# A decoder block's kernel: the order of VectorE's work at the last expert, and of ScalarE's in one attention step

## The chip, the cores and the metric

The kernel runs on one core of a Trainium2 chip. The core has five engines that run programs of their own and meet at semaphores: TensorE (matrix products and transposes), VectorE, ScalarE, GpSimd, and SyncE, which here only issues DMAs. The metric is the time of one execution on the device in microseconds; of several executions the median counts.

## The reference

One layer of a decoder on 512 tokens of width 1024 in float32, then a final normalisation:

```python
h = rms_norm(x, norm_mix) * (1 + sc1) + sh1
x = x + g1 * hybrid_mixer(h, ...)      # four head groups, then @ w_out
h = rms_norm(x, norm_ffn) * (1 + sc2) + sh2
x = x + g2 * hier_moe(h, ...)          # 16 experts, two for each token
out = rms_norm(x, final_norm)
```

The mixer's groups are sliding-window attention (`swa`), causal pooling, an attention with compressed, selected (`sel`) and windowed (`win`) branches, and a gated delta rule. Each expert computes `silu(t @ w_gate) * (t @ w_up)`, times the routing weight, `@ w_down`, with 1024 x 512 weights; a token's two experts are chosen by top-k and the two results are added to the token's row.

## The kernel before, in words

P is 128, ST is 4 (the 512 tokens are four tiles of 128 rows). Each engine's program is written out by hand, in order. An engine waits at `wait_ge` and holds all that stands behind it in its program. `Link` adds a semaphore to an instruction and makes the same engine wait for it.

**The attention** runs in steps s = 0 to 27. A step is one pair of heads and one tile of queries: eight `swa` steps, then sixteen `sel` and `win` steps. At step s TensorE makes the scores of pair s (`pe_attention_step`, L670 and the masks L677), transposes the probabilities of pair s - 2 (L692) and multiplies those of pair s - 3 with the values (L713). VectorE takes the maxima of pair s (L744) and scales the probabilities of pair s - 1 (L769, L772). ScalarE, in `act_attention_step`, makes the exponentials of pair s (L796, L797) and then copies the transposed probabilities of pair s - 2 from PSUM into `pTr` (L809), signalling `pT_out`.

Between steps 9 and 10 (`CMP_TRANSPOSES = 10`) TensorE transposes the probabilities of the compressed branch, `cn` (`pe_cmp_transposes`, L636). They go into the bank that the transposes of the eight `swa` pairs used, so TensorE waits for `pT_out` of all of them, of which the last is copied in ScalarE's step 9. It also waits for `cn`, which VectorE makes (L627). ScalarE copies the result out as `pTc` ahead of its step 10 (`act_cmp_evict`, L641), and TensorE's transposes of the first `sel` pair wait for that. `pe_cmp_values` (L651) uses it at step 11.

**The experts** follow the output projection (L1207) and the routing. Experts are in an order `ORDER`, with n = 0 to 15; they get 128, 64 or 32 rows each, the last three 32. For each n TensorE makes gate and up products (`pe_gate_up`: L1050 for 128 rows, L1044 for fewer), ScalarE applies silu (`act_silu`, L1123, into `sg`), VectorE multiplies with the up half (`dve_product`, L1156 or L1158, into `hidm`), TensorE transposes it (L1060), ScalarE copies it (`act_hidden`, L1128, into `hidT`), and TensorE makes the down products (`pe_down`, L1083 or L1078) with the weights `dn`. Weights come by DMAs that SyncE issues in `sync_moe` (gate and up L913 or L981, down L916) as the three buffers come free. The down weights of the last expert are issued when the down products of the thirteenth (n = 12) are done.

The outputs of experts 0 to 12 are scaled on VectorE and stored to `expert_rows` in HBM. GpSimd gathers them back by token: `y1`, four DMAs that signal `y1_in` together, and `y2`, four DMAs with a signal each (L1701). VectorE adds them, each row times its routing weight, onto `x2` (`rows_added`, L1625, one 128 x 1024 instruction a tile). The outputs of the last three experts stay on the chip: `dve_output` writes them into `yc` (L1172, four pieces), and TensorE's `pe_back` (L1102) multiplies `yc` with a matrix `back` that sends rows to tokens, two halves of 512 columns for each tile. VectorE adds these onto `x2` (L1646), ScalarE squares and sums the tile (L1412) and takes the root (L1414), VectorE scales it (L1676, L1677), and SyncE stores it (L1005), waiting for the stores at the end.

In the loop over experts before the change, VectorE did this for the last one (n = 15): `dve_output` of n = 14, `rows_added` of all four tiles of `y1` and of two of `y2`, `dve_product` of n = 15, the other two tiles of `y2`, and then `dve_output` of n = 15.

Of the kernel before, what the change touches and what calls it, by code (L numbers as in the profile page):

```python
# [45 lines left out]
E = G * EG  # L46
# [215 lines left out]
def build(nc, A, out):  # L262
# [63 lines left out]
    def sem(name):  # L326

        if name not in sems:
            sems[name] = ctx.enter_context(nc.semaphore(name))
        return sems[name]  # L330
# [177 lines left out]
    def pair_heads(kind, pr):  # L508
        return (pr, pr + 2) if kind == "swa" else (2 * pr, 2 * pr + 1)

    def pair_keys(kind, i):

        j0 = max(i - 1, 0) if kind == "swa" else 0
        return j0, (i + 1 - j0) * P
# [260 lines left out]
    Y_DONE = {ST - 1: (0, YBANKS[0]), 2 * ST - 1: (1, YBANKS[1]), 2 * ST + 7: (4, YBANKS[0]), 2 * ST + 15: (5, YBANKS[1])}  # L775
    NUN = 2 * NPS

    def act_attention_step(act, s):
        a = nc.scalar
        if s < NPS:  # L780
            kind, pr, i = pairs[s]
            nk = pair_keys(kind, i)[1]
            for b, n in enumerate(SCORES[s]):
                u = 2 * s + b
                act.wait_ge(sem("max"), u + 1)
                if s >= 2 and b == 0:

                    act.wait_ge(sem("prob"), 2 * (s - 2) + 2)
                if u >= PRS:

                    act.wait_ge(sem("prob_tr"), u - PRS + 1)
                c = 2 * (s % 2) + b
                m = nm[:, c:c + 1]
                if kind == "swa":
                    h = pair_heads(kind, pr)[b]
                    a.activation(esk[:, c:c + 1], sinkb[:, h:h + 1], ACT.Exp, bias=m)  # L796
                a.activation(T["pr"][:, u % PRS, 0:nk], PS[n][:, 0:nk], ACT.Exp, bias=m,  # L797
                             accum_out=den[:, c:c + 1]).then_inc(sem("exp"), 1)
        if TR_LAG <= s < NPS + TR_LAG:
            w = s - TR_LAG  # L800
            kind, pr, i = pairs[w]
            nk = pair_keys(kind, i)[1]
            if w >= 2:

                act.wait_ge(sem("pv_mm"), w - 1)
            for b in range(2):
                act.wait_ge(sem("prob_tr"), 2 * w + b + 1)
                nb = nk // P
                a.activation(T["pTr"][:, w % 2, b, 0:nb, :].rearrange("p j c -> p (j c)"), PROBS[b][:, 0:nk],  # L809
                             ACT.Copy).then_inc(sem("pT_out"), 1)  # L810

    def pe_pool_products(pe, c):

        t = nc.tensor
        pe.wait_ge(sem("wr_in"), 96)
        pe.wait_ge(sem("pool_d"), 2 * c + 2)
        for b in range(2):
            pb = slice(HD * b, HD * b + HD)
            ins = t.matmul(YBANKS[c][pb, :], T["wpool"][pb, c, :], T["pd"][pb, c, :], start=True, stop=True)
        ins.then_inc(sem("pool_mm"), 1)  # L820
# [22 lines left out]
    CMP_SCORES, CMP_IN, CMP_OUT, CMP_TRANSPOSES, CMP_VALUES = 7, 7, 8, 10, 11  # L843
# [49 lines left out]
    def rows_of(n):  # L893
        return SIZES[ORDER[n]] if n < E else P

    def small(n):
        return rows_of(n) < P

    def on_chip(n):
        return E - CHIP <= n < E  # L900

    def down_bank(n):
        return 5 if n == E - 2 else 4
# [237 lines left out]
    def dve_rows(dve, n):  # L1141
        if n:
            dve.wait_ge(sem("mod_moved"), 48)
        scale, shift = (rA, rshift) if n else (A2, mod[:, 24:32])
        dve.wait_ge(sem("xg_tr"), n + 1)
        m = rows_of(n)
        for k in range(4, KT):
            ins = nc.vector.tensor_scalar(T["xgT"][:, k, 0:m], PS[7][:, (k - 4) * m:(k - 3) * m], scale[:, k:k + 1],  # L1148
                                          shift[:, k:k + 1], ALU.mult, ALU.add)
        ins.then_inc(sem("xgT_d"), 1)  # L1150

    def dve_product(dve, n, b):
        dve.wait_ge(sem("sg"), n + 1)
        if small(n):
            f = F * rows_of(n) // P
            ins = nc.vector.tensor_tensor(T["hidm"][:, 0:f], T["sg"][:, 0:f], PS[2 * b][:, f:2 * f], ALU.mult)  # L1156
        else:
            ins = nc.vector.tensor_tensor(T["hidm"][:], T["sg"][:], PS[2 * b + 1][:, :], ALU.mult)  # L1158
        ins.then_inc(sem("hidm"), 1)

    def dve_output(dve, n):

        dve.wait_ge(sem("g2_moved"), 1)
        dve.wait_ge(sem("dn_mm"), n + 1)
        if on_chip(n):

            dve.wait_ge(sem("yo_d"), E - CHIP + 1)
            dve.wait_ge(sem("xg_tr"), E)
            to = slice(32 * (n - E + CHIP + 1), 32 * (n - E + CHIP + 2))
            for w in range(4):  # L1170
                rows, c = slice(32 * w, 32 * w + 32), slice(256 * w, 256 * w + 256)
                ins = nc.vector.tensor_tensor(T["yc"][to, c], PS[down_bank(n)][rows, 0:256], T["g2q"][rows, :],  # L1172
                                              ALU.mult)
            ins.then_inc(sem("yo_d"), 1)
            return
        dve.wait_ge(sem("yo_st"), 16 * STORED[n])
        if small(n):
            d = D * rows_of(n) // P
            g = {512: T["g2s"], 256: T["g2q"]}[d]
            ins = nc.vector.tensor_tensor(T["yo"][:, 0:d], PS[4][:, 0:d], g[:], ALU.mult)  # L1180
        else:
            for w in range(2):
                c = slice(w * 512, (w + 1) * 512)
                ins = nc.vector.tensor_tensor(T["yo"][:, c], PS[4 + w][:, :], T["g2m"][:, c], ALU.mult)  # L1184
        ins.then_inc(sem("yo_d"), 1)
# [230 lines left out]
    def dve_moe(dve):  # L1416
# [200 lines left out]
        def rows_added(n, tiles=range(ST)):  # L1617

            if n == 0:
                dve.wait_ge(sem("y1_in"), 16 * ST)  # L1620
            for i in tiles:
                x = T["x2"][:, i, :]
                if n:
                    dve.wait_ge(sem(f"y_in{i}"), 16)
                ins = v.scalar_tensor_tensor(x, T[f"y{n + 1}"][:, i, :], (w1, w2)[n][:, i:i + 1], x, ALU.mult, ALU.add)  # L1625
            link(ins)

        for n in range(1, E):
            if n == E - 1:
                dve_output(dve, n - 1)  # L1630
                rows_added(0)
                rows_added(1, (0, 1))
            dve_product(dve, n, n % 2)
            if n == E - 1:
                rows_added(1, (2, 3))
            if n + 1 < E:
                dve_rows(dve, n + 1)
                dve_output(dve, n - 1)
            if n == E - 2:
                v.memset(T["yc"][0:32, :], 0.0)  # L1640
        dve_output(dve, E - 1)
        for i in range(ST):
            dve.wait_ge(sem("oproj_mm"), ST + 1 + i + 1)
            for w in range(2):
                x = T["x2"][:, i, w * 512:(w + 1) * 512]
                ins = v.tensor_tensor(x, PS[2 * i + w][:, :], x, ALU.add)  # L1646
            ins.then_inc(sem("x3"), 1)
# [279 lines left out]
    def _(act):  # L1927
# [97 lines left out]
        for s in range(STEPS):  # L2025
            if s == CMP_TRANSPOSES:
                act_cmp_evict(act)
            act_attention_step(act, s)
            if s == HIDDEN_EXP:
                act.wait_ge(sem("gate_in"), 1)  # L2030
                a.activation(gate, gate, ACT.Exp, scale=-1.0).then_inc(sem("scalars"), 1)
                act_compress(act)
            if s == CMP_IN:
                act_cmp_exp(act)
# [5 lines left out]
    def _(dve):  # L2040
# [265 lines left out]
        for s in range(STEPS):  # L2306
# [24 lines left out]
            if s == CMP_OUT:  # L2331
                dve_cmp_softmax_out(dve)
        dve_moe(dve)

    @block.tensor
# [302 lines left out]
```

## Time and profile before

| | us |
|---|---|
| median of 3 runs | 772.02 |
| lowest and highest | 770.45, 775.83 |
| the profiled execution | 771.39 |
| its span, first to last instruction | 769.6 |
| busy in the span: TensorE, VectorE, ScalarE, GpSimd | 682.3, 328.8, 180.2, 116.6 |
| mean granted TensorE clock | 0.957 |

Times in the rows are microseconds from the start of the span. In a row of the chain or of the timeline the first number is the start, the second the length; "x4" counts instructions. A float32 product shows as two or more instructions. "Granted clock" is TensorE's clock as a share of 2.4 GHz; 0.50 is the lower of its two levels, 1.2 GHz.

### The profile page before, as it was taken

To read this page: it belongs to the slowest core of one execution; us is meant where nothing else is said; L and a number is where in the kernel's file an instruction comes from. 1 tells how busy PE (TensorE), PEld (TensorE's weight loads), DVE (VectorE), ACT (ScalarE), POOL (GpSimd) and SP (SyncE) were. 2 spreads that over 40 slices of the span, in tenths; PEclk is the share of its full clock that TensorE was granted. 3 is DMA by queue.
4 is the path that set the end of the run, shared out by engine and by line. 5 is a ranking of instruction groups with operands and counts; after the bars stand their busy time and mean duration, and the time that the engine had idled before them with its cause. 6 is when DMAs were issued, how large, how long until landed. Compare 5 with 4: busy or idle time off the path is not lost.

```text
span 769.6 us, 9939 instructions
## 1 busy us (share of the span) xinstructions
PE 682.3 (89%) x3865; PEld 397.2 (52%) x3869; DVE 328.8 (43%) x782; ACT 180.2 (23%) x435; POOL 116.6 (15%) x164
## 2 busy tenths in 40 slices
PE   1699899999999999887999994899999999999544
PEld 1574346667666598555554554445443444444211
DVE  2203757856467433585723228562111121212355
ACT  3204315122121121455721113111111121111113
POOL 8700122314032057000000000000000000000300
PEclk9999999999999899898999996999999999999977
DMA  9999103793330120850062117998999999999962
GB/s 330 374 258 377 16 1 110 245 311 114 110 110 1 22 35 2 273 187 34 1 219 55 55 37 261 410 327 287 392 403 395 422 397 418 387 413 403 421 261 111
DMA packets 76239, 172.90 MB, mean 225 GB/s; under 512 B 21890, under 2 KB 39004, under 8 KB 72860
## 3 DMA queue, kind: packets, MB, share of 16 engines
q1 hardware_dynamic: 70912, 157.85, 56.6%
q0 software_dynamic: 2608, 9.18, 3.2%
q10 hardware_dynamic: 2668, 5.18, 1.8%
q8 instruction: 33, 0.54, 0.3%
q14 instruction: 18, 0.15, 0.1%
HBM read 156.33 MB, written 15.87 MB: 224 GB/s over the span
## 4 chain that ended last, share of the span: by engine, by line
PE 75%; DVE 11%; POOL 4%; DMA 3%; issue 3%; ACT 3%; POOLq 0%; DVEq 0%; ACTq 0%
PE ps L1050 13%; PE ps L1207 7%; PE ps L2463 7%; PE ps L1083 6%; PE ps L2430 5%; PE ps L1044 5%; PE ps L2541 2%; DMA y<-expert_rows,slot 2%; PE ps L1078 2%; PE ps L2547 2%; PE ps L2427 2%; PE ps L2454 2%; POOL lev L1805 2%; PE ps L2551 2%; PE ps L670 2%
## 5 line engine op out<-in xcount | busy, mean ns | idle before, releaser
L1050 PE MATMUL ps<-gu,xgT 128*128 128x512 f32 x224 | 97.4, 593 | 3.4 <-DVE xgT L1148 2.3
L2463 PE MATMUL ps<-hT,winr 128*128 128x512 f32 x144 | 73.2, 617 | 0.2
L1689 POOL DMA_INDIRECT xg<-xn_rows,list x15 | 13.9, 927 | 381.5 <-PE ps L1019 183.6
L1050 PEld LDWEIGHTS ps<-gu,xgT 128*128 128x128 f32 x224 | 42.0, 190 | 54.1 <-issue 54.1
L1044 PE MATMUL ps<-gu,xgT 128*32 128x256 f32 (+1 forms) x416 | 52.1, 487 | 8.0 <-DMA gu<-in_w_up 8.0
L1207 PE MATMUL ps<-wout,yT 128*128 128x512 f32 x128 | 56.3, 595 | 0.0
L1916 POOL TENSOR_TENSOR cc<-low,lev 128x512 f32<-128x512 f32 x20 | 30.2, 1518 | 131.1 <-DVE low L2250 105.6
L1083 PE MATMUL ps<-dn,hidT 128*128 128x512 f32 x112 | 49.4, 594 | 0.0
L2054 DVE SCALAR_TENSOR_TENSOR acc<-ada,st,acc 128x512 f32<-128x512 f32 x56 | 48.5, 866 | 1.3
L2430 PE MATMUL ps<-hT,wind 128*128 128x512 f32 x96 | 42.3, 594 | 0.0
L1123 ACT ACTIVATE sg<-ps 128x512 f32<-128x512 f32 (+2 forms) x16 | 7.2, 450 | 134.8 <-PE ps L1050 90.5
L1207 PEld LDWEIGHTS ps<-wout,yT 128*128 128x128 f32 x128 | 23.9, 190 | 27.9 <-issue 27.9
L1044 PEld LDWEIGHTS ps<-gu,xgT 128*32 128x32 f32 (+1 forms) x416 | 19.5, 127 | 36.1 <-issue 23.5
L1158 DVE TENSOR_TENSOR hidm<-sg,ps 128x512 f32<-128x512 f32 x7 | 4.8, 686 | 68.6 <-ACT sg L1123 68.6
L1083 PEld LDWEIGHTS ps<-dn,hidT 128*128 128x128 f32 x112 | 20.7, 190 | 23.5 <-issue 23.4
L2463 PEld LDWEIGHTS ps<-hT,winr 128*128 128x128 f32 x144 | 24.4, 195 | 14.7 <-issue 12.7
L744 DVE TENSOR_REDUCE st<-ps 128x1 f32<-128x256 f32 (+3 forms) x48 | 20.4, 452 | 19.0 <-PE ps L677 19.0
L2430 PEld LDWEIGHTS ps<-hT,wind 128*128 128x128 f32 x96 | 17.9, 190 | 20.2 <-issue 20.1
L1078 PE MATMUL ps<-dn,hidT 128*32 128x256 f32 (+1 forms) x208 | 27.4, 498 | 0.7 <-ACT hidT L1128 0.7
L2349 PE MATMUL ps<-ada,st 128*32 128x128 f32 x256 | 11.2, 341 | 18.6 <-DMA ada<-in_w_ada 17.5
L2264 DVE TENSOR_TENSOR uu<-uu,ps 128x512 f32<-128x512 f32 x20 | 13.7, 687 | 32.8 <-PE ps L2547 32.8
L1128 ACT ACTIVATE hidT<-ps 128x512 f32<-128x512 f32 (+2 forms) x16 | 7.2, 451 | 85.4 <-DVE yo L1184 50.5
(451 smaller groups left out, 1083.9 us busy)
## 6 DMA issues: line engine op xcount, KB each, us to landing
dn<-in_w_down SPq DMA_DIRECT2D x16, 2048.0 KB, 20.6
gu<-in_w_gate SPq DMA_DIRECT2D x14, 2048.0 KB, 13.9
gu<-in_w_up SPq DMA_DIRECT2D x14, 2048.0 KB, 19.2
ada<-in_w_ada SPq DMA_DIRECT2D x12, 2048.0 KB, 12.0
expert_rows<-zero SPq DMA_DIRECT2D x12, 512.0 KB, 6.6
gu<-in_w_gate SPq DMA_DIRECT2D x8, 512.0 KB, 5.0
gu<-in_w_up SPq DMA_DIRECT2D x8, 512.0 KB, 6.5
expert_rows<-yo ACTq DMA_DIRECT2D x7, 512.0 KB, 10.5
```

Source lines behind the costliest of these rows:

```text
L670: t.matmul(PS[n][:, 0:nk], q[pb, pr, i * P:(i + 1) * P], keys[pb, 0, j0 * P:j0 * P + nk], start=True, stop=False)
L744: ins = v.tensor_reduce(m, PS[n][:, 0:nk], AX.X, ALU.max, negate=True)
L1044: ins = nc.tensor.matmul(PS[2 * b][m * s:m * s + m, 0:2 * f].rearrange("p (w f) -> p w f", w=2), T["xgT"][:, k, 0:m], w_in[:, :, k, s * f: ...
L1050: ins = nc.tensor.matmul(PS[2 * b + w][:, :], T["xgT"][:, k, :], w_in[:, w, k, :], start=(k == 0), stop=(k == KT - 1))
L1078: ins = nc.tensor.matmul(PS[down_bank(n)][m * w:m * w + m, 0:d], T["hidT"][:, c, m * s:m * s + m], w_in[:, f, w * d:(w + 1) * d], start=(f ...
L1083: ins = nc.tensor.matmul(PS[4 + w][:, :], T["hidT"][:, f, :], w_in[:, f, w * 512:(w + 1) * 512], start=(f == 0), stop=(f == FT - 1))
L1207: ins = nc.tensor.matmul(PS[2 * (i % 2) + n][:, :], T["yT"][:, k, i * P:(i + 1) * P], T["wout"][:, k, n * 512:(n + 1) * 512], start=(k == ...
L1805: link(g.affine_select(out=t, in_=t, pattern=pattern, compare_op=op, fill=fill, base=base, channel_multiplier=cm))
L1916: g.tensor_tensor(CC[lv % 2][:], T["low"][:], T["lev"][:, lv].unsqueeze(1).broadcast_to([P, H, P]), ALU.mult).then_inc(sem("cc"), 1)
L2054: ins = v.scalar_tensor_tensor(o, piece[:, k, :], csil[:, k:k + 1], o, ALU.mult, ALU.add)
L2430: ins = t.matmul(bank[:, :], w(k), T["hT"][:, k, :], start=(k == 0), stop=(k == KT - 1))
L2463: ins = t.matmul(bank[:, :], w(k), T["hT"][:, k, :], start=(k == 0), stop=(k == KT - 1))
```

## The change

ScalarE's attention step is split in two functions, exponentials and copies. Their order is as before in all steps but step 9 (`CMP_TRANSPOSES - 1`), where the copies come first.

On VectorE the last expert's product comes right after the output of expert 14. Tiles 0 and 1 of `y1` are added after it, before the last expert's output; tiles 2 and 3 of `y1` after that output; and each tile of `y2` just ahead of that tile's products from `pe_back`.

```diff
-    def act_attention_step(act, s):
+    def act_exps(act, s):
         a = nc.scalar
         if s < NPS:
...
                 a.activation(T["pr"][:, u % PRS, 0:nk], PS[n][:, 0:nk], ACT.Exp, bias=m,
                              accum_out=den[:, c:c + 1]).then_inc(sem("exp"), 1)
+    def act_prob_copies(act, s):
+        a = nc.scalar
         if TR_LAG <= s < NPS + TR_LAG:
             w = s - TR_LAG
             kind, pr, i = pairs[w]
...
+
+    def act_attention_step(act, s):
+
+        if s == CMP_TRANSPOSES - 1:
+            act_prob_copies(act, s)
+            act_exps(act, s)
+        else:
+            act_exps(act, s)
+            act_prob_copies(act, s)
...
         for n in range(1, E):
             if n == E - 1:
                 dve_output(dve, n - 1)
-                rows_added(0)
-                rows_added(1, (0, 1))
             dve_product(dve, n, n % 2)
-            if n == E - 1:
-                rows_added(1, (2, 3))
             if n + 1 < E:
                 dve_rows(dve, n + 1)
                 dve_output(dve, n - 1)
             if n == E - 2:
                 v.memset(T["yc"][0:32, :], 0.0)
+        rows_added(0, (0, 1))
         dve_output(dve, E - 1)
+        rows_added(0, (2, 3))
         for i in range(ST):
+            rows_added(1, (i,))
             dve.wait_ge(sem("oproj_mm"), ST + 1 + i + 1)
             for w in range(2):
                 x = T["x2"][:, i, w * 512:(w + 1) * 512]
```

## Rows read from the trace of the kernel before

**Rows 1.** The page: DMA share in 40 slices of the span, the chain by engine.

```profile
DMA  9999103793330120850062117998999999999962
...
PE 75%; DVE 11%; POOL 4%; DMA 3%; issue 3%; ACT 3%; POOLq 0%; DVEq 0%; ACTq 0%
```

**Rows 2.** The chain of waits, attention, steps 8 to 12: start, length, what.

```profile
346.41 0.76 DVE cn L627 x2
...
349.26 0.56 ACT pTr L809 x2
...
349.95 1.09 PE ps L636 x4
...
352.09 1.71 PE ps L692 x8
...
356.81 1.24 PE ps L651 x8
...
360.14 0.23 PE ps L692 x2
```

**Rows 3.** The timeline of the same stretch: start, length, what, idle before it and its releaser.

```profile
345.32 0.68 PE L692 MATMUL ps<-idf,pr 128*128 128x128 f32 x4 [0.83 <-ACT pTr L809]
345.94 0.66 PE L713 MATMUL ps<-pTr,va 128*64 128x128 f32 x8
...
348.48 1.00 DVE L772 TENSOR_SCALAR pr<-pr,st 128x512 f32<-128x512 f32 x2
...
351.07 0.60 ACT L641 ACTIVATE pTc<-ps 128x512 f32<-128x512 f32 x1 [1.27 <-PE ps L636]
```

**Rows 4.** Stretches of the attention: busy PE, PEld, DVE, ACT, POOL; granted clock, DMA share, GB/s.

```profile
349.00:350.00 1.00, 0.05 (x1) 0.08 (x2) 0.48 (x2) 0.80 (x4) 0.00 (x0) 0.51 0.00 0
350.00:355.00 5.00, 5.00 (x28) 3.79 (x30) 1.56 (x5) 2.49 (x7) 0.00 (x0) 0.50 0.01 2
```

**Rows 5.** The chain of waits at the end.

```profile
744.24 0.30 DVE hidm L1156
```

**Rows 6.** Timelines of the end, by engine, columns as in rows 3.

```profile
720.55 1.93 PE L1078 MATMUL ps<-dn,hidT 128*32 128x256 f32 x32 [0.36 <-ACT hidT L1128]
...
736.30 0.28 ACT L1123 ACTIVATE sg<-ps 128x128 f32<-128x128 f32 x1 [15.81 <-PE ps L1044]
736.82 4.87 DVE L1625 SCALAR_TENSOR_TENSOR x<-y,w1t,x 128x1024 f32<-128x1024 f32 x4 [12.14 <-DMA y<-expert_rows,slot]
...
745.42 3.37 PE L1078 MATMUL ps<-dn,hidT 128*32 128x256 f32 x32 [0.37 <-ACT hidT L1128]
...
749.02 1.73 DVE L1172 TENSOR_TENSOR yc<-ps,g2q 32x256 f32<-32x256 f32 x4 [2.10 <-issue]
...
759.73 1.29 DVE L1646 TENSOR_TENSOR x<-ps,x 128x512 f32<-128x512 f32 x2 [0.43 <-PE ps L1102]
```

**Rows 7.** The chain of waits later in the attention, at a granted clock of 1.00.

```profile
375.54 0.59 PE ps L713 x8
376.13 0.42 PE ps L670 x4
376.55 0.22 PE ps L677 x2
376.77 0.88 PE ps L692 x8
377.65 1.02 PE ps L713 x16
378.67 0.85 PE ps L670 x4
```

**Rows 8.** The timeline of SyncE: the issue of the last down weights.

```profile
713.64 0.38 SPq L916 DMA_DIRECT2D dn<-in_w_down  x1
```

**Rows 9.** DMA issues between 713.5 and 714.0: KB, us from issue to landing.

```profile
dn<-in_w_down SPq DMA_DIRECT2D x1, 2048.0 KB, 26.6
```

**Rows 10.** A stretch of the end, columns as in rows 4.

```profile
741.00:742.00 1.00, 0.00 (x0) 0.00 (x0) 0.96 (x2) 0.00 (x0) 0.00 (x0) 0.78 1.03 410
```

## The prediction

> **What bounds the kernel now.** I read the chain of waits first. TensorE has three quarters of it and VectorE a tenth [rows 1]; so an edit on VectorE or ScalarE pays only where TensorE stands waiting for that engine. The change touches two such places, far apart, and the reader should look at each on its own.
>
> The first is the step of the attention before TensorE's transposes of the compressed probabilities. In the chain [rows 2] TensorE's four transposes (L636) start at 349.95, released by ScalarE's two copies (L809), which ended at 349.82. Their other input, `cn`, was finished by VectorE at 346.41 + 0.76 = 347.17. The probabilities that the copies move had been transposed by 345.32 + 0.68 = 346.00 [rows 3]. ScalarE held the copies back because its program has the exponentials of that step ahead of them, and these waited for maxima. TensorE's pause made its clock fall: granted 0.51 in the microsecond from 349, and 0.50 from 350 to 355 [rows 4], the lower of its two levels (1.2 against 2.4 GHz).
>
> The second is the end. The chain [rows 5] has the product `hidm` of the last expert at 744.24, though its input `sg` was ready at 736.30 + 0.28 = 736.58 [rows 6]. Between them VectorE added gathered rows `y`, from 736.82, when the first of them had landed. Then come TensorE's down products at 745.42, `yc` on VectorE until 749.02 + 1.73 = 750.75, the products that send rows back to their tokens, the last addition until 759.73 + 1.29 = 761.02, the final scalings and the stores. From 761.02 to the end of the span (769.6) are 8.58 us, which the change leaves alone.
>
> **Part one: copies before exponentials in one step.** Nothing is added or removed; ScalarE exchanges two exponentials and two copies at step 9. The copies need the transposes that ended at 346.00. Moved up they run while ScalarE waits for maxima, and by their own 0.65 us or so are over near 346.7, a microsecond before the exponentials can begin. So the exponentials keep their time, and no queue of DMAs is passed.
> TensorE's L636 can then start at about 347.2, when `cn` is there: 2.7 us earlier. What is late next? The transposes of the selected probabilities (L692, behind L636 and two score products) wait for ScalarE's copy `pTc`. That copy stands in ScalarE's queue behind step 9's exponentials, which end where the copies began, at 349.26 [rows 2]. It takes 0.60 us [rows 3], so L692 starts at about 350.0. VectorE's probabilities for it are done by 348.48 + 1.00 = 349.5 [rows 3]. Before, L692 followed its predecessors in TensorE's queue at 352.09 by the chain, or 351.9 with the overlap of single records. That is 1.9 us, and it is carried on, since TensorE works without a gap from there to 360.14.
> There is more if the clock stays up. The work from L692 to the row at 360.14 is, by the same shapes at the full clock [rows 7] : transposes 0.88, values 0.59, scores 0.42 + 0.22, transposes 0.88, the compressed values 1.24 (the row at 356.81 in [rows 2], run mostly after the clock had risen), values 1.02, scores 0.85 + 0.22: together 6.3 us, so 356.3 instead of 360.14, a gain of 3.8 us. The other engines follow: ScalarE's exponentials of step 10 and its copies, and VectorE's maxima and scalings, each come out ready before TensorE asks. Does it stay up? TensorE stopped at 345.94 + 0.66 = 346.6 [rows 3], and a granted 0.51 from 349 to 350 means that the clock fell at about 349.0, after 2.4 us of standing still. With the change the pauses are 0.6 us (346.6 to 347.2) and 1.5 us (about 348.5 to 350.0). I take the full clock, 3.8 us, and keep 1.9 as the bound. The lowest bound is 0, if the 1.9 us were lost to a wait that I do not see; a loss has no row, since ScalarE idles where the copies go. After this place all waits are between engines that move together: the output products, the routing, and the loads of expert weights, which SyncE issues on signals of TensorE and VectorE. So the gain arrives at the end whole.
>
> **Part two: the product first.** VectorE does the same 8 additions of gathered rows, one product, four pieces of `yc`, and 8 half additions. Only their order changes.
> Removed from the path: the additions between 736.82 and 744.24. The product could start at 736.6. From product to down products were 745.42 - 744.24 = 1.18 us, so TensorE could begin them at 737.8.
> A new wait takes the place: the down weights of the last expert. Their DMA was issued at 713.64 [rows 8] and landed 26.6 us later [rows 9], at 740.24. Before, that was hidden. Now the down products start at about 740.3, 5.1 us earlier than before and not 7.6.
> Their length depends on the clock. The same 32 products took 1.93 us at 720.55 and 3.37 us at 745.42 [rows 6], the latter at the lower level: in the trace the clock fell to it between 741 and 742 [rows 10], some 5.3 us after the last gate and up product, which ended as `sg` began. In the new order one transpose (0.3 to 0.5 us) comes at about 737.0 and then 2.8 us without work, close to the 2.4 us after which the clock fell in the attention and well under the 5.3 us here. Rows leave this open, so I take the middle of the two.
> From the end of the down products to the end of `yc` were 750.75 - 748.79 = 1.96 us. So `yc` is ready at 740.3 + 1.93 + 1.96 = 744.2, or at 740.3 + 3.37 + 1.96 = 745.6; before 750.75.
> Now the additions that used to lie ahead stand behind: two of the first rows (1.22 us each, 4.87 for four in [rows 6]), then for each of four tiles one of the second rows (1.22 too, and some 0.06 for the waits around a single one) and two halves (1.29). 2 x 1.22 + 4 x (1.22 + 0.06 + 1.29) = 12.7 us, all on VectorE, one after another. TensorE's back products all fell in the 10.3 us from `yc` to the last addition, so VectorE becomes the bound of the tail. Two additions of first rows are hidden in the wait for the weights. Before, `yc` to the last addition took 761.02 - 750.75 = 10.3 us; it will take 2.4 us more, because six additions of rows are behind it.
> End of the span for this part alone: 744.2 + 12.7 + 8.6 = 765.5 or 745.6 + 12.7 + 8.6 = 766.9, against 769.6: a gain of 4.1 or 2.7, middle 3.4. ScalarE's squares (about 1.1 us a tile) keep up with 2.6 us a tile. Its table load at 745.6 moves forward with `hidT` and is off the path.
>
> By the Trainium skill (TensorE: Matmul & The Clock Gate, Part 1) the gate judges TensorE's activity on a schedule that runs on its own and does not begin with the kernel, so the place of a fall differs between executions. The two falls here (2.4 and 5.3 us after the last work) agree with that. If so, the tail's clock is a draw in each execution rather than one value. Its two outcomes are those priced above, 765.5 and 766.9.
>
> **Sum.** 3.8 + 3.4 = 7.2 us. The profiled execution took 771.39 us for its span of 769.6; it should become 762.4 in the span and 764.2 in all. The median of the runs shown, 772.02, is 0.6 above it, so I forecast 764.8.
>
> **Rivals.**
> (A) As above, 763.4 to 765.9 with the clock and small hops. Chance 0.58.
> (B) The clock falls in the attention all the same, so that part brings 1.9: 766.7. For it: TensorE still works only about half of the time between 344.4 and 350. Against it: no single pause is as long as that of before. 0.17.
> (C) The edit in the attention does not do what it says, because L636 or L692 is held by something that the copies hid: 0 + 3.4, 768.6. For it: only a last releaser is shown. Against it: `cn` was there at 347.17. 0.12.
> (D) DMA is the pace of the expert stage and not TensorE. The DMA engines are at nine tenths and more from routing on [rows 1], and nothing of what they move gets less. The attention's gain is then used up in waits for weights, and the last down weights may come when the old down products began, 745.4, or later. Then `yc` is done at 750.75 as before, with 12.7 us behind it where 10.3 were: 772.02 + 2.4 = 774.4, slower. The tail turns into a loss once the down products start after 769.6 - 8.6 - 12.7 - 1.96 - 3.37 = 743.0. Against it: SyncE issues each load on a release, which comes earlier with the rest; the landing would have to slip by 2.7 us. 0.05.
> (E) In most executions the last down weights land before 737.8, so nothing holds them: 2.4 us more, 762.4. For it: I have one execution. 0.08.
>
> **How the numbers follow.** A measurement of this kernel can tell about 1% (7.7 us) from no change, so the forecast lies almost on that line, 764.3. A has about two fifths of its chance under it, E all of its own, B a little through the scatter of runs (770.45 to 775.83): faster 0.36. Slower by over 1% needs D and more: 0.04. The rest, 0.60, is within 1%. The range: 761.8 (E, with some scatter) to 768.9 (C), which leaves out D, the far side of E and part of C.
>
> **What would show it.** In the profile after: ScalarE's copies of step 9 at about 346 and L636 at about 347.2; L692 at about 350; granted clock 1.00 through 350 to 355 (B: 0.50); everything from L1207 on 3.8 us earlier. At the end, in distances: the product within 0.1 us of `sg`; TensorE's down products 3 to 4 us after the end of the last gate and up products, released by the DMA of `dn`; the half additions one after another on VectorE with no idle time, about 2.6 us a tile, while TensorE is done before. If the down products start 1.2 us after `sg`, E holds. If L1207 starts at 391.6 as before, C does. The prediction goes wrong above all if the landing of the last down weights moves against TensorE's work, for each microsecond there is one of the result.

## The result, and the profile after

Over 20 executions of each the changed kernel took 768.12 us (median; 762.40 to 772.09), the kernel before 773.49 (766.13 to 777.91). The ratio is 0.9945, with a 95% interval of 0.9927 to 0.9964: 4.2 us less, between 2.8 and 5.6. The forecast was 7.2 less. The profiled execution of the changed kernel took 767.23 us, span 765.4, against 771.39 and 769.6. Lines of the changed kernel from L797 on have other numbers (L809 is now L811, L1207 is L1218, L1078 is L1089).

The attention first: the chain of waits of the changed kernel (start, length, what), against [rows 2].

```profile
343.52 0.76 DVE cn L627 x2
...
346.37 0.50 ACT pTc L641
...
347.00 1.06 PE ps L692 x8
...
353.57 0.23 PE ps L692 x2
```

And its timeline, with the moved copies (343.22) and TensorE's transposes of `cn`:

```profile
343.22 0.66 ACT L811 ACTIVATE pTr<-ps 128x256 f32<-128x256 f32 x2 [0.65 <-PE ps L692]
...
344.34 0.65 PE L636 MATMUL ps<-idf,cn 128*128 128x128 f32 x4 [0.41 <-DVE cn L627]
```

The copies are over before VectorE has finished `cn`, L636 starts 0.06 us after it (before: 2.78 us after), and L692 waits for `pTc`, as worked out. From the end of `cn` to the row that was at 360.14 were 12.97 us, and now are 9.29: 3.68 less. The clock stayed up; busy PE, PEld, DVE, ACT, POOL, then the granted clock, in the stretch where [rows 4] has 0.50:

```profile
350.00:355.00 5.00, 5.00 (x52) 2.92 (x52) 2.44 (x9) 2.23 (x8) 0.00 (x0) 1.00 0.01 3
```

Now the end, in the timelines of VectorE and TensorE of the changed kernel, against [rows 6]:

```profile
735.23 0.29 DVE L1167 TENSOR_TENSOR hidm<-sg,ps 128x128 f32<-128x128 f32 x1 [9.72 <-ACT sg L1134]
735.44 2.48 DVE L1636 SCALAR_TENSOR_TENSOR x<-y,w1t,x 128x1024 f32<-128x1024 f32 x2
742.34 1.73 DVE L1183 TENSOR_TENSOR yc<-ps,g2q 32x256 f32<-32x256 f32 x4 [4.42 <-issue]
...
755.49 1.29 DVE L1656 TENSOR_TENSOR x<-ps,x 128x512 f32<-128x512 f32 x2
...
728.67 6.17 PE L1055 MATMUL ps<-gu,xgT 128*32 128x256 f32 x64 [5.33 <-DMA gu<-in_w_up]
735.58 0.33 PE L1071 MATMUL ps<-idf,hidm 128*128 128x128 f32 x1 [0.73 <-DVE hidm L1167]
738.49 3.64 PE L1089 MATMUL ps<-dn,hidT 128*32 128x256 f32 x32 [2.58 <-issue]
744.21 8.72 PE L1113 MATMUL ps<-yc,back 128*128 128x512 f32 x16 [2.09 <-DVE yc L1183]
```

The row to look at is the one at 738.49. The product follows `sg` at once, but TensorE stands idle for 2.58 us between its transpose of `hidm` and the down products. "Issue" names no one: the profile sees no engine that released them. Their weights had been issued at 711.79, and the view of DMA issues gives 26.6 us to landing, 738.4. `yc` is done at 744.07, and then VectorE works without a pause to 755.49 + 1.29 = 756.78.

Both local forecasts hold in what happens, and nearly in size, and yet the sum does not. The ledger of the two profiles, in us, from the starts and ends of the same instructions:

| distance | before | after | less |
|---|---|---|---|
| start of the span to the end of `cn` | 347.17 | 344.28 | 2.89 |
| `cn` to the first product of the output projection | 44.41 | 40.74 | 3.67 |
| from there to the issue of the first down weights | 68.28 | 69.98 | -1.70 |
| to the first expert's gate and up products | 26.98 | 26.97 | 0.01 |
| to the last expert's gate and up products | 243.68 | 246.70 | -3.02 |
| to VectorE's last addition | 30.50 | 28.11 | 2.39 |
| to the end of the span | 8.58 | 8.62 | -0.04 |
| sum | 769.6 | 765.4 | 4.20 |

The -0.04 in the last row is rounding: the spans are given to a tenth. The first row has identical code in both kernels and cannot be the change's. The clock's falls lie elsewhere in the two executions: granted 0.54 from 260 to 264 us before and 1.00 after, 0.52 and 0.83 from 315 to 322. The third and fifth are losses in places that the edit does not touch, and they need an explanation. In the timeline of the changed kernel the first expert's products take 16.99 us, where the kernel before has 13.97:

```profile
481.97 16.99 PE L1061 MATMUL ps<-gu,xgT 128*128 128x512 f32 x32 [2.06 <-DVE xgT L1159]
```

```profile
486.84 13.97 PE L1050 MATMUL ps<-gu,xgT 128*128 128x512 f32 x32 [2.32 <-DVE xgT L1148]
```

The windows of the changed kernel show the granted clock (third number from the end) in the output projection and in these products:

```profile
436.00:437.00 1.00, 1.00 (x6) 0.74 (x6) 0.26 (x2) 0.64 (x3) 0.00 (x0) 0.93 0.00 0
437.00:440.00 3.00, 3.00 (x4) 1.01 (x3) 1.05 (x1) 0.00 (x0) 0.00 (x0) 0.50 0.37 147
440.00:441.00 1.00, 1.00 (x3) 0.49 (x2) 0.00 (x0) 0.00 (x0) 0.00 (x0) 0.87 0.25 98
...
481.00:487.00 6.00, 5.03 (x6) 2.18 (x7) 5.59 (x27) 0.00 (x0) 1.19 (x1) 0.52 0.97 410
```

TensorE's products run on in both, at half its clock: 3.4 us at the lower level in the projection cost 1.7, some 6 us in the expert's products cost 3.0. In the profile of the kernel before the clock is 1.00 in both places.

### The profile page after: what moved, and what is told of

Read it like the earlier page. It is cut to its first block, busy times and chain, and to the rows that moved or that the text cites. A ratio compares the mean times of both kernels' runs of the same rounds, so it can differ in the third digit from the quotient of the medians.

```text
span 765.4 us, 9942 instructions
## 1 busy us (share of the span) xinstructions
PE 686.4 (90%) x3865; PEld 397.8 (52%) x3869; DVE 330.2 (43%) x782; ACT 180.7 (24%) x435; POOL 116.8 (15%) x164
## 4 chain that ended last, share of the span: by engine, by line
PE 75%; DVE 11%; POOL 4%; issue 3%; DMA 3%; ACT 3%; SPq 0%; POOLq 0%; DVEq 0%; ACTq 0%
PE ps L1061 13%; PE ps L1218 7%; PE ps L2473 7%; PE ps L1094 6%; PE ps L1055 6%; PE ps L2440 5%; DMA gu<-in_w_up 3%; PE ps L2551 2%; PE ps L2557 2%; PE ps L1089 2%; PE ps L2437 2%; PE ps L2464 2%; POOL lev L1815 2%; PE ps L670 2%; PE ps L2561 2%
## 5 line engine op out<-in xcount | busy, mean ns | idle before, releaser
L1061 PE MATMUL ps<-gu,xgT 128*128 128x512 f32 x224 | 100.5, 608 | 3.1 <-DVE xgT L1159 2.1
L1218 PE MATMUL ps<-wout,yT 128*128 128x512 f32 x128 | 58.0, 610 | 0.0
L1218 PEld LDWEIGHTS ps<-wout,yT 128*128 128x128 f32 x128 | 24.4, 195 | 29.0 <-issue 29.0
L1089 PE MATMUL ps<-dn,hidT 128*32 128x256 f32 (+1 forms) x208 | 29.3, 504 | 3.8 <-issue 3.2
L1167 DVE TENSOR_TENSOR hidm<-sg,ps 128x256 f32<-128x256 f32 (+1 forms) x9 | 3.3, 362 | 58.5 <-ACT sg L1134 58.5
L1441 DVE TENSOR_TENSOR x<-ps,g1b 128x512 f32<-128x512 f32 x8 | 5.5, 689 | 49.3 <-PE ps L1218 49.3
## 6 DMA issues: line engine op xcount, KB each, us to landing
gu<-in_w_gate SPq DMA_DIRECT2D x14, 2048.0 KB, 13.2
```

Of the source, the lines that this page charges most:

```text
L1061: ins = nc.tensor.matmul(PS[2 * b + w][:, :], T["xgT"][:, k, :], w_in[:, w, k, :], start=(k == 0), stop=(k == KT - 1))
L1089: ins = nc.tensor.matmul(PS[down_bank(n)][m * w:m * w + m, 0:d], T["hidT"][:, c, m * s:m * s + m], w_in[:, f, w * d:(w + 1) * d], start=(f ...
L1218: ins = nc.tensor.matmul(PS[2 * (i % 2) + n][:, :], T["yT"][:, k, i * P:(i + 1) * P], T["wout"][:, k, n * 512:(n + 1) * 512], start=(k == ...
```

## The experiments

"Faster" and "less" are against executions of the kernel before that were taken beside those of the run, unless said. One microsecond is 0.0013 of the ratio.

**The two edits apart** (`e1_copies_only`, `e2_product_only`): each takes one hunk of the diff alone.

> The attention's edit alone (copies ahead of exponentials in step 9, VectorE's order as before). Theory T1, terms as predicted: 3.8 us less than before, ratio about 0.995. Theory T2, clock draws: the 1.9 us from waits are there in every execution, but the further 1.9 us need that the kernel before has its fall of the clock in that pause; over many executions that holds in part, and the time is 2 to 3 us less, ratio 0.996 to 0.9975. Rival T3, the expert stage eats it: 0 to 1 us. In the profile under T1 and T2: TensorE's transposes of cn start when cn is done, and the span between cn and the output projection is shorter by 3.5 us than in the profile of before, at a full clock.

Measured: 768.18 against 771.16; ratio 0.9955 (0.9930 to 0.9980), 3.5 us less. The distance from `cn` to the projection is 40.75 in its profile. The expectation's T1 fits the median; the interval holds T2 as well, and shuts T3 out.

> VectorE's edit alone (product of the last expert first, step 9 of ScalarE as before). Theory: down products start when the last down weights land, VectorE then has 12.7 us from yc to the last addition: 2.4 to 2.7 us less than before with the low clock in the down products, 4.1 with the full clock; ratio 0.9945 to 0.997. Rival: the serial additions cost all that the earlier product brings, 0 us. If the two edits add, the ratio of this run and that of the other edit give together 0.9945, the ratio of the whole change.

Measured: 769.65; 0.9974 (0.9947 to 1.0001), 2.0 us less, not clear of zero by itself. The two together would be 0.9929, the whole change 0.9945 (0.9927 to 0.9964): they add, within what can be told. The new tail is not all VectorE's either: with the back products at the low clock from start to end (10.09 us) TensorE held up two of the half additions, and from `yc` to the last addition it took 13.2 us and not 12.7. The old tail is itself not one number. In the first run, with VectorE's old order, the gate and up products to the last addition took 28.88 us and not 30.50, because TensorE's back products ran at the full clock from the start:

```profile
749.23 7.10 PE L1113 MATMUL ps<-yc,back 128*128 128x512 f32 x16 [2.10 <-DVE yc L1183]
```

**More additions ahead** (`e3_five_ahead`), to see whether VectorE is the bound of the tail:

```diff
-        rows_added(0, (0, 1))
+        rows_added(0)
+        rows_added(1, (0,))
         dve_output(dve, E - 1)
-        rows_added(0, (2, 3))
         for i in range(ST):
-            rows_added(1, (i,))
+            if i:
+                rows_added(1, (i,))
```

> The changed kernel, but all four tiles of y1 and the first of y2 are added in the wait for the last down weights, so three additions (3.7 us) leave the stretch behind yc. Theory (VectorE bounds the tail): 2 to 3 us less than the changed kernel, because TensorE's back products then become the bound at about 10.3 us from yc to the last addition, as before the change; against before 6 to 7 us less, ratio 0.991 to 0.992. Rival (the tail is bound by something else, or yc is delayed by the additions ahead): no gain over the changed kernel, ratio 0.9945, or a loss of 1 us.

Measured: 767.12; 0.9942 (0.9918 to 0.9966). No gain over the changed kernel; the expectation was wrong. The timeline of VectorE shows why:

```profile
742.11 1.73 DVE L1183 TENSOR_TENSOR yc<-ps,g2q 32x256 f32<-32x256 f32 x4 [0.63 <-PE ps L1089]
747.67 1.29 DVE L1657 TENSOR_TENSOR x<-ps,x 128x512 f32<-128x512 f32 x2 [3.83 <-PE ps L1113]
748.88 1.28 DVE L1636 SCALAR_TENSOR_TENSOR x<-y,w2t,x 128x1024 f32<-128x1024 f32 x1
```

The time saved behind `yc` became a wait of 3.83 us for TensorE's first back products, and three additions of `y2` still stood between the half additions after it. From the start of the back products to the last addition it took 12.52 us, and 12.57 in the changed kernel. VectorE and TensorE each bound pieces of this tail.

**A lighter load of the last down weights** (`e4_light_down`):

```diff
-                load_down(sp, expert[n - 1], (n - 1) % NBUF)
+                if n == E:
+                    sp.dma_start(dn[..][:, 0:1], wd_v[expert[n - 1]][:, 0:1]).then_inc(..)
+                else:
+                    load_down(sp, expert[n - 1], (n - 1) % NBUF)
```

> The changed kernel with only the first quarter of the last expert's down weights loaded (the other three quarters are left out, so the last expert computes with old weights there). Theory (the landing of these weights starts the down products): they start 1.2 us after sg instead of 3.5 us, and the time is 2.2 to 2.5 us less than that of the changed kernel, ratio to before about 0.9915. Rival (down products wait for something else on ScalarE or VectorE): they start as late as in the changed kernel, and the ratio stays at 0.9945.

Measured: 763.82; 0.9917 (0.9883 to 0.9950). In its profile the down products are released by ScalarE's `hidT`, with no other wait, 1.44 us after the gate and up products and not 3.65:

```profile
737.02 1.93 PE L1093 MATMUL ps<-dn,hidT 128*32 128x256 f32 x32 [0.37 <-ACT hidT L1143]
```

The last gate and up products to the last addition took 23.99 us instead of 28.11. Of these 4.1 us 2.2 are the wait, and 1.7 the down products, which ran at the full clock. Over executions it is 2.1 us less than the changed kernel, by the ratios. The landing was the wait.

**TensorE kept at work in the tail** (`e5_busy_tail`): `pe_busy(n)` issues n spare transposes of 128x128 into a bank that nobody reads.

```diff
         pe_hidden(pe, E - 1, 1)
+        pe_busy(20)
         pe_down(pe, E - 1)
+        pe_busy(15)
```

> The changed kernel with 20 spare transposes on TensorE between the last expert's hidden transposes and its down products, and 15 between down products and back products, into a bank that nobody reads. Theory (the clock falls in these pauses and nothing else in the tail is sensitive to it): the down products take 1.9 us instead of 3.6, so yc and the end come 1.7 us sooner than in the changed kernel; the back products get shorter too (8.8 to 7 us), which brings nothing, as VectorE's additions are the bound. Ratio to before about 0.9925. Rival (the fall has another reason, or the spare work delays the down products): ratio 0.9945 or more.

Measured: 764.19 against 770.68; 0.9920 (0.9894 to 0.9945). Down products 1.93 us, back products 7.10; gate and up products to the last addition 26.36, that is 1.75 less than in the changed kernel: 1.71 is what the fall cost the down products. Over executions it is 1.9 us, with intervals that overlap. Back products to the last addition stayed at 12.56: VectorE's bound, whatever TensorE's clock.

**Additions in both gaps** (`e7_adds_in_gaps`), the lesson of the run with five ahead, and the same with the spare work of the tail (`e8_gaps_and_busy`):

```diff
-        rows_added(0, (0, 1))
+        rows_added(0)
+        rows_added(1, (0,))
         dve_output(dve, E - 1)
-        rows_added(0, (2, 3))
+        rows_added(1, (1, 2, 3))
         for i in range(ST):
-            rows_added(1, (i,))
```

> The changed kernel, with all of y1 and the first tile of y2 added in the wait for the down weights, and the other three tiles of y2 in the wait for the first back products, where VectorE stood idle for 3.8 us in the run with five additions ahead. Theory: nothing but half additions is left behind TensorE's back products, so these bound the tail: from yc to the last addition 10.3 us instead of 12.7, and 2.4 us less than the changed kernel at the low clock, up to 4 at the full clock. Ratio to before 0.9905 to 0.9915. Rival (VectorE is no bound): ratio 0.9945.

Measured: 762.14 against 770.68; 0.9876 (0.9839 to 0.9914), clearly faster than the kernel before. Gate and up products to the last addition 26.99 us in its profile, 1.1 less than the changed kernel; the waits that VectorE has left are TensorE's, whose back products took 10.12 us at the low clock (from `yc` to the last addition 11.6 us, where 10.3 were expected):

```profile
745.60 3.68 DVE L1636 SCALAR_TENSOR_TENSOR x<-y,w2t,x 128x1024 f32<-128x1024 f32 x3
749.57 1.29 DVE L1656 TENSOR_TENSOR x<-ps,x 128x512 f32<-128x512 f32 x2 [0.30 <-PE ps L1113]
752.43 1.29 DVE L1656 TENSOR_TENSOR x<-ps,x 128x512 f32<-128x512 f32 x2 [1.57 <-PE ps L1113]
```

By the ratios it is 5 us less than the changed kernel, and the profile accounts for 1.1 of them. The six executions had a mean granted clock of 0.964, against 0.956 for the kernel before; why theirs was so high is not shown, so the size of this gain is open.

> Both of the last two ideas in the tail: additions in the gaps and TensorE kept at work. Theory: now the back products are the bound, and their clock counts: 1.7 us from the down products and 1.5 to 1.8 us from the back products on top of the run with additions in the gaps, so 3 us less than that, ratio to before 0.987. Rival (spare work brings only the down products' 1.7 us, or nothing): 0.989 to 0.991.

Measured: 761.68; 0.9864 (0.9824 to 0.9905). The profile has what was expected, 23.41 us for that distance, 3.6 less than without the spare work. Over executions the two cannot be told apart (six of each).

**Spare work in the attention's pause of the kernel before** (`e6_busy_pause`):

```diff
     def pe_cmp_transposes(pe):
         t = nc.tensor
+        pe.wait_ge(sem("exp"), 2 * SWA_STEPS + 2)
+        for j in range(24):
+            t.transpose(SPARE[:, (j % 4) * P:(j % 4 + 1) * P], idf[:], idf[:])
```

> The kernel before, with 24 spare transposes on TensorE in the pause ahead of L636, into a bank that is free by then. L636 itself starts where it did. Theory (half of the attention's gain is the clock): the clock no longer falls there, and the work up to the output projection is 1.9 us shorter than in the profile of before; over executions 1 to 1.9 us, ratio 0.9975 to 0.9985. Rival (all of the gain is the shorter wait): ratio 1.000.

Measured: 771.07 against 770.68; 1.0011 (0.9989 to 1.0033). The profile has the gain, `cn` to projection 42.23 us and not 44.41; and it has a fall in the projection, 69.98 and not 68.28, which takes 1.7 of the 2.2 back. Over executions nothing is left, and the granted clock says the same: its mean is 0.9566 over these 12 executions and 0.9564 over the 23 of the kernel before. A fall spared and not made up for, 6.8 us at half the clock as in the profile of before, would have raised it by 0.0044 (an estimate, 6.8 x 0.5 / 770).

**Two more profiles of each kernel** (`r1_before_again` to `r4_after_again`).

> The kernel before once more, for its profile. Theory (each execution has its own places where the clock falls, and distances without a fall are fixed): from cn to the first output product 44.4 us with the fall in the pause, or 42.2 without it; from there to the first down load 68.3, 70.0 or 71.6 us, with no, one or two short falls in the output projection; start of the first gate and up products to the last 243.5 or 246.5. If over the profiles of before all of these are drawn, the clock's places are chance and not a result of the edit. Rival: before always has 44.4, 68.3 and 243.5, and only kernels with the earlier copies have the later falls; then the edit itself moves the falls and pays its gain back.

> As for the first repetition of the kernel before: a second draw of the same distances.

> The changed kernel once more, for its profile. Theory: from cn to the first output product always 40.7 us; the output projection 68.3, 70.0 or 71.6 and the experts 243.5 or 246.5 by chance; the last down products 3.64 us long in most executions, and from the end of yc to the last addition 12.7 us whatever the clock. Rival: output projection always 70.0 or more.

> As for the first repetition of the changed kernel: a second draw of the same distances.

Their times were 771.65 and 766.89 (before), 767.09 and 767.20 (after). All profiles without spare work in the projection or at the first expert:

| kernels | to `cn` | `cn` to projection | projection | first to last expert |
|---|---|---|---|---|
| before, three profiles | 347.2, 347.4, 343.3 | 44.41, 44.42, 43.67 | 68.28 in all | 243.7, 243.8, 244.0 |
| VectorE's edit alone | 347.6 | 44.42 | 68.28 | 243.4 |
| before, busy pause | 346.2 | 42.23 | 69.98 | 243.5 |
| after, three | 344.3, 345.8, 344.2 | 40.74 in all | 69.98, 71.64, 69.97 | 246.7, 243.5, 246.8 |
| other kernels with the earlier copies, six | 344.2 to 347.4 | 40.73 to 40.77 | 69.97 (four), 71.64, 71.65 | 246.4 to 247.2 (five), 243.5 |

Every profile with the earlier copies pays 1.7 or 3.4 us in the projection, and seven of nine pay 3.0 at the first expert. No profile of the old order pays anything, but for the one with the busy pause. That is the rival of these four runs, not their theory. Nor does "12.7 us whatever the clock" hold for every new tail: where the back products take about 10 us it is 13.1 to 13.2 (VectorE's edit alone, and the two runs with spare work below that leave the tail as it is).

Could the profiles with the earlier copies merely have been taken in executions of another kind? Three pairs of profiles rule that out for the projection. The kernel before and the run with additions in the gaps run the same code up to step 9, finished `cn` at 347.17 and 347.23, and up to there their clock was at the lower level in the same four stretches, to within 0.1 us. The only difference between `cn` and the projection is the order of step 9. Windows of the kernel before, then of the run with additions in the gaps:

```profile
349.00:356.00 7.00, 6.05 (x35) 4.64 (x36) 2.21 (x8) 3.29 (x11) 0.00 (x0) 0.51 0.01 4
420.00:428.00 8.00, 6.83 (x34) 4.36 (x33) 3.99 (x6) 2.53 (x5) 0.00 (x0) 1.00 0.23 86
```

```profile
349.00:356.00 7.00, 6.05 (x58) 4.05 (x58) 3.78 (x13) 4.46 (x15) 0.00 (x0) 1.00 0.01 4
420.00:428.00 8.00, 8.00 (x22) 4.66 (x22) 1.62 (x3) 1.45 (x3) 0.00 (x0) 0.57 0.37 132
```

The fall at 349 is gone, and one at 420.7 has come, in the 20-column products behind the projection's first wait; in the kernel before these products run 3.6 us later, at 1.00. The first repetition of the kernel before and the run with spare work in the tail are such a pair too, and so are VectorE's edit alone and the run below with spare work at the first expert. For the fall at the first expert only the second of the three pairs shows it.

**Spare work where the clock fell** (`e9_busy_expert0`, `e10_busy_projection`, `e11_before_busy_both`, `e12_all`):

```diff
             all_transposes(i - 1)
+            pe_busy(9, 6)
             all_logits(i - 1)
...
+        pe_busy(17)
         pe_gate_up(pe, 0, 0)
```

> The changed kernel with 17 spare transposes on TensorE in the wait ahead of the first expert's gate and up products (about 2 us where it stands idle). In seven of nine profiles with the earlier copies the clock is at the lower level in the first part of these products, which costs 3.0 us; in none of four profiles of the old order. Theory (the fall comes from that pause and the edit's shift made it likely): start of the first to start of the last gate and up products 243.5 us in the profile, and 2 to 2.5 us less than the changed kernel over executions, ratio 0.991 to 0.992. Rival (chance of the profiles alone): ratio 0.9945.

Measured: 765.88 against 770.02; 0.9937 (0.9913 to 0.9961). First to last expert 244.45 in its profile. It points the right way by 0.6 us, but is not to be told from the changed kernel. Nor does its profile decide: two profiles without this spare work (one of the changed kernel, and the run with additions in the gaps) also had two falls in the projection and none here.

> The changed kernel with nine spare transposes in each of two waits of the output projection, between TensorE's transposes of x2 and the products with the routing weights. In all nine profiles with the earlier copies the clock falls once or twice after such a wait, 1.7 or 3.4 us, in none of four of the old order. Theory: the fall comes from that stretch, and with work in the wait the projection takes 68.3 us; 1.7 to 2.2 us less than the changed kernel, ratio 0.992. Rival (the routing products themselves, 20 columns wide, are the cause): 70.0 us as before the spare work, ratio 0.9945.

Measured: 764.71; 0.9930 (0.9905 to 0.9954). In its profile the projection took 68.28 us, the only kernel with the earlier copies, beside the one with all spare work, where it did. The spare transposes fill a wait of one microsecond, and the output products behind the routing products run at 7.11 us, where the changed kernel had 8.81:

```profile
436.56 1.15 PE L1100 MATMUL ps<-idf 128*128 128x128 f32 x9
437.90 1.96 PE L1255 MATMUL ps<-wrA,x2T 128*128 128x20 f32 x16 [0.19 <-ACT x2T L1361]
439.71 7.11 PE L1222 MATMUL ps<-wout,yT 128*128 128x512 f32 x16
```

```profile
434.43 1.96 PE L1251 MATMUL ps<-wrA,x2T 128*128 128x20 f32 x16 [1.18 <-ACT x2T L1356]
436.24 8.81 PE L1218 MATMUL ps<-wout,yT 128*128 128x512 f32 x16
```

The first fence is the run with spare work, the second the changed kernel. Over executions it is 1.2 us better than the changed kernel by the ratios, with intervals that overlap.

> The kernel before with the spare work of both other runs. Theory (the edit's shift moves the falls there, the old order is free of them): nothing to gain, ratio 1.000. Rival (the old order has these falls as often, its profiles just did not show them): the same gain as the changed kernel has from both, ratio 0.994 to 0.996.

Measured: 770.11 against 770.02; 0.9989 (0.9967 to 1.0012). The same spare work brings the kernel before at most 2.5 us, and likelier nothing. Its profile has 68.27 and 243.18, as without it. The one with spare work at the first expert has no fall there, but two in the projection (71.64).

> The run with additions in the gaps and spare work in the tail, plus spare work in the projection and ahead of the first expert. If the gains add: 4 us less than without the last two, ratio to before about 0.981. Rival: 0.986, as without them.

Measured: 760.25; 0.9858 (0.9823 to 0.9894), the fastest kernel here, 10.9 us under the one before by the ratio. Its profile agrees: it finished `cn` at 347.26, as the kernel before did at 347.17, and its span is 758.4 against 769.6. Over executions the last two edits add next to nothing: 0.981 was forecast, 0.9864 is the value without them.

## Why the prediction was wrong, point by point

**The attention's part, where it is made: right.** Its terms gave 3.8 us; 3.67 was measured; all twelve profiles with the earlier copies have 40.73 to 40.77 us for that distance. L636 starts when `cn` is ready, L692 when `pTc` is, and the clock stays up.

**"So the gain arrives at the end whole": this step failed.** I had checked that all waits behind it are between engines that move together, and they are: the distance from the first down weights to the first expert was 26.95 to 27.0 us in all profiles. The loads did not eat the gain either, against rival D: from the loads issued during the first expert's products on SyncE issues every load 1.85 us earlier in the changed kernel's profile (488.84 against 490.69, and still 711.79 against 713.64 for the last). What I left out, and so put at nothing, is that TensorE's clock does not move along with the work. In the three pairs of profiles above, the same up to step 9, the projection comes 3.6 us earlier and one fall is spared, and the clock falls in a stretch of it that had run at 1.00. Which of the two brings the new fall, the shift or the fall spared, no run separates. In the profile the changed kernel was 6.6 us ahead where the projection begins (2.9 and 3.7) and 1.9 ahead at the last expert; 4.7 are gone. That keeping the clock up in one pause can be paid back later is shown by the busy pause: it gained 2.2 us there, lost 1.7 in the projection, and over executions brought nothing, neither in time nor in granted clock.

How much of it over all executions? The copies alone brought 3.5 us, between 1.5 and 5.4, which leaves room for all of the 3.8 and for half of it. Their mean granted clock rose by 0.0027 (0.9578 against 0.9551), where the fall in the pause alone, spared for good, is worth 0.0044: by this estimate, which has a scatter of its own, some of it comes back and not all. That the later falls follow from the edit rests on the pairs, on the other profiles (in the projection ten of ten without spare work there, the run with it at the first expert among them, against none of four) and on spare work that takes the fall away there and brings the kernel before nothing; the gain of that spare work over executions was not clear of zero. The profiles reach `cn` between 343.3 and 347.7 us with the same code up to there, and differ in where the clock falls on the way; what chooses the places is not settled. The scatter of one kernel's times goes with the clock: of the 29 executions of the kernel before that stand beside the copies alone, the five fastest (766.1 to 769.3 us) had a mean granted clock of 0.960, the five slowest (774.5 to 775.2) of 0.950.

**The tail: mechanism right in the main, size too large.** The new wait for the down weights was found, its landing of 26.6 us too, and it was the wait. VectorE as the bound with 12.7 us behind `yc` was 12.71 (744.07 to 756.78). The term that was mis-sized is the clock of the down products: I took the middle of two outcomes, and of the eight profiles of the new tail with the full load and no spare work there six have the low one, 3.64 us, and two fall on the way (2.95 and 3.04). So 2.7 and not 3.4; the profile has 2.39, for at the lower level throughout they take 3.64 us, and the 3.37 that I used had run in part above it. And the old tail, my base of 30.50 us, is TensorE's and varies with its clock (28.88 in one profile, 30.3 to 30.6 in the five others), while the new one varies less: 12.7 us behind `yc` where VectorE is the bound, 13.1 to 13.2 in the three profiles of this order where the back products took about 10 us. That TensorE could still hold VectorE up I had not foreseen. VectorE's edit alone measured 2.0 us.

**The sum.** 7.2 was forecast, 4.2 measured (2.8 to 5.6). About one of the missing three is the tail's, by the profile (1.4 by the run with VectorE's edit alone). In the profile the falls of the clock take back 4.7 us, more than the attention's part, and only the 2.9 us that the execution was ahead at `cn`, where the code is the same, bring its sum near the measured gain: that is luck. Over executions the rest, 4.2 less the tail's 2.0 to 2.4, leaves some 2 us for the attention's part; that lies in the lower half of what the copies alone measured, and the two edits measured apart come to 5.5, so its share is not known to better than a microsecond or two.

**The rivals.** B did not come: granted 1.00 from 350 to 355. C's price was near (768.6), for another reason: the edit did what it says. D's worry, loads as the pace, was not borne out; its arithmetic of the tail was right. E needed weights that land before 737.8, and by the run with a lighter load it would have been worth 4.1 us in a profile, with the down products at the full clock, and 2.1 over executions, near the 2.4 that I gave it. The Trainium skill (TensorE: Matmul & The Clock Gate, Part 1) had the point that I weighed in the prediction: the gate's schedule does not begin with the kernel, so the place of a fall is not fixed by the kernel alone. The profiles agree: of three of the kernel before two have the attention's fall 1.8 us after the end of `cn`, the third has a shorter one 4.4 us after it, when L636 was already running. I applied it to the tail and not to everything behind the attention.

## What to carry to other kernels

A gain is made at one place and read at the end; between them lie all stretches in which TensorE is nearly idle or does narrow work, and a shift or a fall avoided can bring a new fall of its clock there, as it did here. So compare distances between the same instructions over several profiles before calling a local gain the kernel's. When work is moved off the path, look for every gap that could take it: five additions in the first gap alone brought nothing over the change, five there and three in the next gap did (1.1 us in the profile, more over executions). And a load that was hidden behind a late instruction is the first thing to look up when that instruction moves forward.

## What was unexpected of the hardware

TensorE's clock fell inside a stage in which TensorE is busy nine tenths of the time: after 1.04 us of transposes, a wait of 1.18 us and 1.96 us of products 20 columns wide, the next output products ran 3.4 us at the lower level (8.81 us for what takes 7.11). The same three pieces also pass without a fall, in all profiles of the kernel before. The distances between instructions are otherwise so exact (0.04 us over the twelve profiles with the earlier copies) that such a fall shows as steps of 1.70 us: 68.28, 69.98, 71.65.
